# Modulation blocks of a diffusion layer: two of six parts at the head, the other eight blocks inside the attention's head pairs

## The reference

```python
mod = SiLU(cond) @ w_mod[l] + b_mod[l]          # 1024 x 6144 weights per layer, 2 conditioning vectors
sh1, sc1, g1, sh2, sc2, g2 = split(mod, 6)
h   = x * (1 + sc1) + sh1                       # before the input projection
...                                             # recurrence over 8 heads, attention over 16 heads
x   = layer_norm(ALPHA * x + g1 * (y @ w_out))
h2  = x * (1 + sc2) + sh2                       # input of the mixer of experts
x   = layer_norm(ALPHA * x + g2 * peer_mixer(h2))
```

## Time and profile before

| | us |
|---|---|
| median of 3 runs | 6148.52 (6143.78 to 6161.4) |
| the profiled execution's own time | 6114.04 |
| its span in the profile | 6112.2 |
| PE busy | 5046.7 (83%) |
| DVE busy | 3742.0 (61%) |
| ACT busy | 825.7 (14%) |
| POOL busy | 1726.2 (28%) |
| mean DMA rate over the span | 260 GB/s |

### The profile page before, as it was taken

How to read it: one execution, slowest core, us unless ns; L and a number is a source line. 1 busy time by engine, 2 the same in 40 slices (tenths; PEclk the granted TensorE clock), 3 DMA queues, 4 the chain that set the end, 5 groups by cost and what they waited for, 6 DMA issues and landing times. The chain is left out here.

```text
span 6112.2 us, 62289 instructions
## 1 busy us (share of the span) xinstructions
PE 5046.7 (83%) x18696; PEld 2745.5 (45%) x18696; DVE 3742.0 (61%) x7541; ACT 825.7 (14%) x2126; POOL 1726.2 (28%) x1567
## 2 busy tenths in 40 slices
PE   5998789897977777777769987998979777777776
PEld 3787367643432222222237873676434322223222
DVE  0366333378888787876604663323788787878665
ACT  0121033000111001010101210330001110010100
POOL 0000000055644444443300000000657444444432
PEclk8999889998999999999989988899989899999999
DMA  6111100487999999999941111014979999999997
GB/s 230 45 47 46 46 1 27 180 331 296 385 373 400 409 403 411 398 416 421 368 179 45 46 46 46 1 43 177 346 295 379 374 407 409 403 412 396 416 421 328
DMA packets 251837, 1589.74 MB, mean 260 GB/s; under 512 B 28849, under 2 KB 38705, under 8 KB 105649
## 3 DMA queue, kind: packets, MB, share of 16 engines
q0 software_dynamic: 221184, 1342.28, 54.8%
q1 hardware_dynamic: 15936, 224.93, 9.6%
q10 hardware_dynamic: 14448, 19.42, 0.9%
HBM read 1581.27 MB, written 5.24 MB: 260 GB/s over the span
## 5 line engine op out<-in xcount | busy, mean ns | idle before, releaser
L751 PE MATMUL banks<-arena 128*128 128x512 f32 x1152 | 652.0, 649 | 304.4 <-PEq L1208 302.3
L365 POOL DMA_INDIRECT arena<-in_peer_uv,eidx x512 | 563.2, 1100 | 738.7 <-POOLq L364 708.8
L1646 DVE SCALAR_TENSOR_TENSOR arena<-arena 128x1024 f32<-128x1024 f32 x512 | 626.8, 1224 | 146.3 <-DMA arena<-in_peer_uv,eidx 133.7
L346 POOL DMA_INDIRECT arena<-in_peer_uv,eidx x512 | 592.5, 1157 | 335.9 <-POOLq L345 203.3
L753 PE MATMUL banks<-arena 128*128 128x512 f32 x1152 | 615.9, 617 | 0.0
L332 POOL COPY late<-arena 128x640 f32 x16 | 11.4, 719 | 1875.5 <-POOLq L331 1875.5
L417 ACT ACTIVATE late<-late 128x1 f32<-128x1 f32 (+1 forms) x1026 | 208.3, 203 | 2374.3 <-ACTq L416 2374.1
L751 PEld LDWEIGHTS banks<-arena 128*128 128x128 f32 x1152 | 202.0, 201 | 710.2 <-issue 709.8
L751 PE MATMUL banks<-ring,arena 128*128 128x512 f32 x512 | 301.1, 672 | 238.5 <-PEq L1208 238.5
L825 PE MATMUL banks<-hT,ring 128*128 128x320 f32 x1536 | 432.5, 433 | 2.9 <-PEq L822 2.9
L365 POOL DMA_INDIRECT ring<-in_peer_uv,eidx x256 | 286.3, 1118 | 477.3 <-POOLq L364 454.5
(11 more groups left out here) (255 smaller groups left out, 7312.1 us busy)
## 6 DMA issues: line engine op xcount, KB each, us to landing
ring<-in_wblk SPq DMA_DIRECT2D x106, 2048.0 KB, 7.9
arena<-in_peer_uv,eidx POOLq DMA_INDIRECT x1024, 9.0
arena<-in_lnrows ACTq DMA_DIRECT2D x6, 1024.0 KB, 8.2
arena<-in_sk ACTq DMA_DIRECT2D x4, 1024.0 KB, 9.0
hT<-in_peer_uv,eidx POOLq DMA_INDIRECT x256, 11.9
ring<-in_peer_uv,eidx POOLq DMA_INDIRECT x256, 12.3
x<-in_x_sample ACTq DMA_DIRECT2D x1, 2048.0 KB, 18.3
late<-in_state ACTq DMA_DIRECT2D x32, 64.0 KB, 1.8
```

What stands on the lines that cost most here:

```text
L346: nc.gpsimd.indirect_dma_start(grow[j], None, ins["peer_uv"], bass.IndirectOffsetOnAxis(ap=eidx[:, n, r:r + 1].bitcast(U32), axis=0)).then ...
L365: nc.gpsimd.indirect_dma_start(gslot[j], None, ins["peer_uv"].rearrange("(e h) d -> e (h d)", h=2), bass.IndirectOffsetOnAxis(ap=eidx[:, n ...
L751: nc.tensor.matmul(banks[:, 4, :], diag[n], row[:, 0:CB], start=start, stop=stop, skip_group_check=True).then_inc(diag_used, 1)
L1646: V.scalar_tensor_tensor(u, u, 1.0, h2[:, t - 1, :], ALU.mult, ALU.mult, accum_out=av[:, r:r + 1])
```

## The change

`modrows` now holds four blocks instead of twelve, so the head of a layer handles SH1 and SC1 alone. The other eight `w_mod` blocks come behind the Q blocks in the order of the weights (`B_PART` 17), and each head pair of the attention takes one: in step 3, after the scores and before `weigh`, PE waits for the block, runs its 32 matmuls into columns 384 to 511 of bank 7, drains and frees the slot. DVE copies the result to `laterows` ahead of each `normalise`. After the attention PE turns these rows with two groups of four transposes, DVE adds the biases, and `spread` stands behind the mix blocks instead of ahead of them; the context's two `w_out` blocks write to banks 0 and 1 instead of 4 and 5. At the start of the program the conditioning vectors are loaded first, under a semaphore of their own, and ACT's SiLU and PE's first blocks no longer wait for `init`.

```diff
-B_MOD, B_GATE, B_HEAD, B_KV, B_Q, B_MIX, B_OUT, B_PQ = 0, 12, 14, 22, 23, 25, 33, 35
+B_MOD, B_GATE, B_HEAD, B_KV, B_Q, B_PART, B_MIX, B_OUT, B_PQ = 0, 4, 6, 14, 15, 17, 25, 33, 35
-        modrows = arena[:, 0:12 * P]
+        modrows = arena[:, 0:4 * P]
+        laterows = reg.take(8 * P)
...
+            act.dma_start(cond[:], ins["cond"]).then_inc(cond_full, 16)
...
+            act.wait_ge(cond_full, 16)
+            nc.scalar.activation(cond[:], cond[:], ACT.Silu).then_inc(cond_ready, 1)
             act.wait_ge(init, INIT)
-            nc.scalar.activation(cond[:], cond[:], ACT.Silu).then_inc(cond_ready, 1)
...
             pe.wait_ge(rows_zero, 1)
-            pe.wait_ge(init, INIT)
             pe.wait_ge(cond_ready, 1)
...
+                pe.wait_ge(init, INIT)
                 pe.wait_ge(modrows_ready, 1)
                 pe.sem_inc(modrows_ready, -1)
-                for b in range(3):
...
+                turn_parts(modrows, 0, 2)
...
+                def mod_part(s):
+                    pe.wait_ge(w_full[s], 16)
+                    pe.sem_inc(w_full[s], -16)
+                    mod_block(s, banks[:, 7, 3 * P:4 * P])
+                    pe.drain().then_inc(w_free[s], 1)
...
+                        if u == 3:
+                            mod_part((B_PART + b) % 2)
                         if u:
                             weigh(b, u - 1)
...
-                for v, part in enumerate((G1, SC2, SH2)):
-                    spread(4 + 2 * (v % 2), part, 0)
+                for b in range(2):
+                    turn_parts(laterows, 4 * b, 2 + b)
                 for n in range(KD):
...
+                pe.wait_ge(modv_ready, 1)
+                pe.sem_inc(modv_ready, -1)
+                for v, part in enumerate((G1, SC2, SH2)):
+                    spread(4 + 2 * (v % 2), part, 0)
                 pe.wait_ge(y_ready, KD)
...
                     dve.wait_ge(to_dve[6], 1)
                     dve.sem_inc(to_dve[6], -1)
+                    V.tensor_copy(laterows[:, bass.ds(p * P, P)], banks[:, 7, 3 * P:4 * P])
                     V.reciprocal(psum[b], psum[b])
...
+                add_bias(2, 16)
+                add_bias(3, 32, SC2)
+                dve.drain().then_inc(modv_ready, 1)
```

More of the change, by code:

```diff
@@ L608, in _ @@
                                          ).then_inc(sg_ready[n % 2], 1)
+                for v in range(3):
+                    copy_out(bc_ctx[:, v], 4 + 2 * (v % 2))
+                act.drain().then_inc(bc_ready, 1)
                 square_root(1)
@@ L762, in _, with mod_block @@
             pe.wait_ge(rows_zero, 1)
-            pe.wait_ge(init, INIT)
             pe.wait_ge(cond_ready, 1)
             with pe.Fori(0, DEPTH) as l:
+                def mod_block(s, out):
+                    for k in range(KD):
+                        for j in range(4):
+                            last = nc.tensor.matmul(out[32 * j:32 * j + 2, :], cond[:, k, :],
+                                                    ring[:, s, k, j * P:(j + 1) * P],
+                                                    start=k == 0, stop=k == KD - 1)
+                    return last
                 with pe.Fori(0, B_GATE // 2):
@@ L1316, in _, with add_bias @@
                 dve.drain().then_inc(modrows_ready, 1)
[L1317 to L1326, removed]
+                def add_bias(b, first, scales=None):
+                    dve.wait_ge(to_dve[b], 1)
+                    dve.sem_inc(to_dve[b], -1)
+                    V.tensor_tensor(modv[:, first:first + 16, :], r3(banks[:, b, :], 32)[:, :, 0:2],
+                                    bmod[:, bass.ds(l, 1), first:first + 16].rearrange("p a m -> p (a m)")
+                                    .unsqueeze(2).to_broadcast([P, 16, 2]), ALU.add).then_inc(bank_free[b], 1)
+                    if scales is not None:
+                        dve.drain()
+                        V.tensor_scalar(modv[:, scales * 8:scales * 8 + 8, :], modv[:, scales * 8:scales * 8 + 8, :],
+                                        1.0, None, ALU.add)
+                add_bias(2, 0, SC1)
                 phase_barrier(dve, "dve")
@@ L1493, in att_pair @@
                             lowest(1 - b, u + 2 - 2 * NT)
[L1494 to L1495 removed]
+                        if u == 0 and before is not None:
+                            normalise(1 - b, before)
                 for u in range(2):
                     lowest(0, u)
[L1499 to L1504, removed]
+                att_pair(0, None, True)
+                with dve.Fori(0, QH // 4 - 1) as i:
+                    att_pair(1, 2 * i, True)
+                    att_pair(0, 2 * i + 1, True)
+                att_pair(1, QH // 2 - 2, False)
+                normalise(1, QH // 2 - 1)
                 phase_barrier(dve, "dve")
+                add_bias(2, 16)
+                add_bias(3, 32, SC2)
+                dve.drain().then_inc(modv_ready, 1)
                 def first_level(source, a, b):
@@ L1784, in layout @@
     for l in range(DEPTH):
-        blocks = [a["w_mod"][l][:, j * CB:(j + 1) * CB] for j in range(12)]
+        blocks = [a["w_mod"][l][:, j * CB:(j + 1) * CB] for j in range(4)]
         blocks += [hg[l][:, j * CB:(j + 1) * CB] for j in range(2)]
@@ L1788, in layout @@
         blocks += [np.concatenate([ak[l], av[l]], 1), aq[l][:, 0:CB], aq[l][:, CB:]]
+        blocks += [a["w_mod"][l][:, j * CB:(j + 1) * CB] for j in range(4, 12)]
         blocks += [np.concatenate([w[l][:, n * P:(n + 1) * P] for w in (ga, gb, a["w_branch_rec"], watt)], 1)
```

33 lines of the change are left out of this document (14 added, 19 removed).

## The result

The changed kernel takes 6077.3 us (median of 4 runs, 6067.72 to 6087.4), against 6154.96 us for the kernel before (4 runs, 6143.78 to 6162.59). The forecast was 6077.

A forecast was written before the change was run, and what follows sets the result against it. It took the heads as bound by DMA loads and the attention by PE; -58.6 - 55.2 + 38.1 + 4.6 = -71.1 us, taken from the median 6148.5, gave 6077 us, range 6058 to 6106.

The forecast's parts named there:

- The head of layer 0: Start to layer 0's gate projection: eight blocks and the SiLU's wait go, gate at 51.17 instead of 109.74, saving 58.6 us.
- The early start of 6.35 us: Layer 0's first block starts 6.35 us earlier as the SiLU needs only the conditioning vectors; bounds 0 and 6.35.
- Rival D: In layer 0 `init` still decides, the 6.35 us are lost: 6084 us; counted within the forecast's 80% chance.
- The head of layer 1: Layer 1's first block stays at 3067.70, its gate projection starts at 3099.36 instead of 3154.56, saving 55.2 us.
- The attention: Each of 16 head pairs gains matmuls, drain and a DVE copy: 38.1 us plus 4.6 us added in all.
- The drain: In each head pair, 0.45 us on PE from the part's end to the next work, beside 1.93 of matmuls.
- is ended by time: Each pair's low-clock stretch ends by time, not work done, so the part was taken at 1.93 us.
- Rival A: Attention parts run at the low clock without giving it back: 26.7 us more, 6104 us; chance 13%.
- Rival B: Each attention part pulls the clock down and a low stretch follows: 56.3 us more, 6133 us; chance 4%.
- Rival C: Clock stays low from each attention part to the next output: 392 us more, 6469 us, slower than before; chance 3%.
- The context part: From the spread to `w_out` after the attention: counted 0, bounds -1.9 and +1 us per layer.
- The sum: All terms over the kernel: -71.1 us against the profiled 6114.0, so 6042.9; on the median 6077 us.

The follow-up runs named there:

- e6: Changed kernel with the SiLU of the conditioning vectors behind `init` again; 6039.31 us in a single run, 70.3 under its session's kernel before.
- e1: Kernel before, unedited, run and profiled again on one chip with the changed kernel; median 6105.31 us of 9 timed runs.
- e2: Changed kernel, unedited, run and profiled again beside the kernel before on one chip; 6034.48 us, ratio 0.9881 to before.
- e3: Changed kernel with each head pair's part cut to 4 of its 32 matmuls, four of six parts then being incomplete; 6025.85 us in one run.
- e5: Changed kernel with the 32 matmuls of every part run twice, on another chip; 6067.73 us, 41.9 under that session's kernel before.
- e9: Kernel before with 32 useless matmuls of the part's form added in its 1.70 us wait; 6075.66 us against 6108.95, ratio 0.995.

## Why the forecast was right, step by step

**The head of layer 0: right.** Fourth block forecast at 37.48, found at 37.67; gate at 51.17, found at 52.33. Two terms were off and small. The fourth block took 3.39 us where I had taken the warm 1.93 from the row at 43.83, and the way from its end to the gate took 11.27 instead of 11.76. The early start of 6.35 us came at the fourth block almost whole (43.83 against 37.67, so 6.2), and the slower fourth block took 1.5 of it back; e6 gives 5.3 at the gate. Rival D (`init` still decides) falls with the gate: at 57.74 with the SiLU behind `init` (e6), at 52.44 without, and with ACT's row, where the SiLU starts at 18.74 without a wait.

**The head of layer 1: right in kind, its size depends on the execution.** Forecast 55.2; 56.9 in the first profiles, 48.4 from e1 to e2. The forecast of the new head, 31.7 us, was good (30.0 and 31.6 found). What moved is the head of before that it was taken from: 86.9 us in the first profile, 80.0 in e1. Two things are in these 6.9. The pace of the loads from the fourth to the twelfth block was 6.46 us per block and 6.12 in e1, which makes 2.7 us. The other 4.1 us lie behind the start of the last block: in e1 it and the turns after it ran at the full clock (1.93 and 1.50 us in the rows above), in the first profile at the low one (3.60; the 12 transposes 2.79). After the change this part behind the fourth block's end is 10.1 us in both profiles, where 11.70 was forecast, and the fourth block itself took 1.93 in one and 3.59 in the other. So one execution is not enough to price a stretch of short bursts: its clock alone moved by 4 us.

**The attention: right in sign and mechanism, the sizes partly off.** Forecast 2.67 us per pair (1.93 + 0.45 + 0.29), found 2.48 at equal clock, 2.37 in the last whole pair. The matmuls are there with 1.93 (e3 and e5 confirm 1.5 for 56 records and 1.74 for 64), the copy with 0.31 (0.20 in the last whole pair, where the output's wait grew to 0.59 only). The drain was mis-sized: I took the 0.45 us between two blocks at the head, and between the part and the `weigh` behind it 770.57 - 768.38 - 1.93 = 0.26 are lost. With 0.26 in its place the terms add up to what was found, 2.50 and 2.39. The pair of 37.3 that I named is found only in three pairs of six.

Per layer the eight parts and drains make 17.5 us at equal clock, and the longer waits of the eight outputs 2.3, together 19.8; measured are 19.1 (first profiles) and 17.7 (e1 to e2), where 21.4 was forecast. So from e1 to e2 1.5 of the miss is the drain and 2.1 the clock, which I had left as it was. These 2.1 are the rest of larger shifts that cancel: the six whole pairs grew by 9.4 us where 14.9 is due at equal clock, and the piece behind them by 5.6 where 2.4 is due (its clock was 1.00 in e1 and 0.89 in e2). In before's first profile five of the six whole pairs have the low stretch, in e1 all six, in after three have a whole one, two a half and one none. That the low stretch "is ended by time", and not made longer by the part, held only so far: five of the eight parts of layer 0 took 1.93 us, and three ran partly in it (2.29, 2.45 and this one):

```profile
732.31 2.55 PE L774 MATMUL banks<-ring,cond 128*2 128x128 f32 x64
```

Rival A wanted each part at 3.60; the longest was 2.57. Rival B wanted a low stretch behind every part; the first pair's window behind its part (770.60 to 774.00) shows 1.00, and the rows behind the other parts have the short durations (e9 shows the opposite effect of such matmuls, if they fill a wait). Rival C is out by the pairs of 33.7 to 37.0 us.

**The context part: 0 forecast, and found near it by errors that cancel.** From the last output to `w_out` it took 74.10 us instead of 75.55 in the first profiles, and 74.42 instead of 74.11 from e1 to e2. In it:

```profile
1034.52 3.81 PE L1089 MATMUL banks<-hT,ring 128*128 128x128 f32 x32 [1.65 <-PEq L1086]
...
1075.62 5.59 PE L740 MATMUL banks<-ident,modv 128*128 128x128 f32 x48 [0.41 <-PEq L738]
1081.05 7.03 PE L727 MATMUL banks<-ring,arena 128*128 128x512 f32 x16
```

The spread takes 5.59 instead of 8.33, but that is no work of the change: at its old place it took 5.59 in e1 too.

```profile
1050.67 5.59 PE L735 MATMUL banks<-ident,modv 128*128 128x128 f32 x48 [1.39 <-PEq L733]
```

`w_out`'s first block takes 7.03 instead of 8.80, in both pairs of profiles. It now follows dense work without a wait, as the lower bound of -1.9 supposed. Against that three mix blocks wait 1.2 to 2.1 us for their loads (1.65, 1.45 and 1.48 in the first profile), where before had one such wait and e1 two. Why their loads come late was not tried.

**The sum.** -71.1 forecast, -71.6 from e1 to e2. Part of the hit is luck: the gain of layer 1's head was forecast 6.8 us too large (55.2 against 48.4), and the loss in the attention 7.2 us too large (42.7 against 17.7 + 17.8), and the two cancel. Against the first pair of profiles the sum would have looked 37 us wrong, but these two are hardly a true pair, as said above, and the medians of the first session say -77.7. That the median came out at 6077.3 is luck as well: 6077 was -71.1 from a median of 6148.5, and with the fourth run of before this median is 6154.96.

The Trainium skill ("TensorE: Matmul & The Clock Gate", section "HAM oscillation — how this bites in real kernels") describes the oscillation as one of bursts separated by waits. The traces agree at the heads, where a block behind a wait of 7.09 us took 3.59 us instead of 1.93. The attention shows it with much shorter waits: in e1 the single wait of 1.70 us in an otherwise dense stream was followed by a low stretch in six of six whole pairs, and filling it removed all of them (e9). It isn't followed by one always. The same wait stands in the piece behind the sixth pair of e1, whose clock is 1.00, and in one pair of six of after. What decides this is open.

## What to carry to other kernels

Moving work from a stretch bound by DMA into one bound by PE is priced by two rows, the pace of loads in the first and the duration of the matmuls in the second; it paid here at 6 us against 2.5 per block, with the DMA idle in the second stretch. Then look for the place in the dense stream: at equal clock the same matmuls cost 2.5 us per pair in the middle of it and 0.6 to 0.9 in a wait (31.93 and 32.24 against 31.34) that is there anyway. There they hold the clock as well, which was worth more (2.1 us per pair) than the time that they save by lying in the wait (1.6). Compare lengths of a repeated piece at equal granted clock before you put a difference down to work, look whether the waits at its two ends are the same, and take the two profiles on one chip and in one session before you add up stretches.

## What the runs showed that I had not expected

- More matmuls, less time: 32 useless ones in a 1.70 us wait made a pair 2.9 us shorter and the kernel 0.5% faster (e9).
- Fewer matmuls, lower clock: with an eighth of the part's matmuls two pairs of six in layer 0 and one in layer 1 dropped to a granted clock of 0.82, against 0.91 at the lowest with all of them (e3). Which pairs get a low stretch was the same in both executions of after and not quite in those of before (five and six of six); what decides it is open.
- The gap that a drain leaves on PE between two dense pieces was 0.26 to 0.29 us ahead of `weigh`, and 0.41 to 0.45 where transposes or another block of two columns follow. Waits for semaphores stand in the second kind too, and what each adds was not tried.
- The same head of twelve 2 MB blocks took 86.9 us in one execution and 80.0 in another, more of it by the clock behind the last block than by the loads. The latent part with its query blocks took 230 to 233 us or 260 to 264, the long ones in the session in which both kernels were over 40 us slower. Such a stretch can move by more between two sessions than the attention does by the change.
